# Cache pages of a paged attention in a ring of six group buffers instead of seven

## The reference

```python
PAST_LEN, PAGE_SIZE, DEC_BATCH = 2048, 128, 8
N_HEADS, KV_LORA, QK_ROPE = 8, 512, 64

def mla_sample_attn(q_abs, q_pe, c_new, kpe_new, c_pool, kpe_pool, page_table, w_uv):
    c_past = c_pool[page_table].reshape(dbs, -1, KV_LORA)
    kpe_past = kpe_pool[page_table].reshape(dbs, -1, QK_ROPE)
    s_past = (einsum('bqhr,bkr->bhqk', q_abs, c_past)
              + einsum('bqhe,bke->bhqk', q_pe, kpe_past)) * SOFTMAX_SCALE
    ...
    w = softmax(concatenate([s_past, s_new], axis=-1))
    o_lat = einsum('bhqk,bkr->bqhr', w[..., :n_past], c_past) + einsum(..., c_new)
    return einsum('bqhr,rhv->bqhv', o_lat, w_uv)
```

## Time and profile before

| | us |
|---|---|
| runs before: median of 3 (lowest to highest) | 1185.36 (1183.1 to 1186.95) |
| profiled execution, its own time | 1187.33 |
| its span, first to last instruction | 1185.6 |
| PE busy | 1095.9 |
| DVE, ACT, POOL busy | 590.3, 384.8, 139.0 |
| mean granted PE clock (share of full speed) | 0.971 |

### The profile page before, as it was taken

How to read it: one execution, slowest core, us unless ns; L and a number is a source line. 1 busy time by engine, 2 the same in 40 slices (tenths; PEclk the granted TensorE clock), 3 DMA queues, 4 the chain that set the end, 5 groups by cost and what they waited for, 6 DMA issues and landing times.

```text
span 1185.6 us, 25393 instructions
## 1 busy us (share of the span) xinstructions
PE 1095.9 (92%) x9906; PEld 1016.8 (86%) x9906; DVE 590.3 (50%) x1245; ACT 384.8 (32%) x761; POOL 139.0 (12%) x220
## 2 busy tenths in 40 slices
PE   2899949999999999999789989899999989999995
PEld 2899949999999999989789987677767668999995
DVE  5466432543288851367675436655555552232332
ACT  6331111121133221144551231445444442232333
POOL 0000020000050000010421710123322200000000
PEclk9899978999999999999899989999999999999998
DMA  9443493233344344135535864657777687323213
GB/s 272 100 128 97 127 104 84 76 91 90 90 129 124 98 135 123 63 106 181 157 117 155 256 191 149 204 170 230 219 208 224 197 254 252 107 71 103 74 35 144
DMA packets 199445, 169.99 MB, mean 143 GB/s; under 512 B 35595, under 2 KB 164022, under 8 KB 197526
## 3 DMA queue, kind: packets, MB, share of 16 engines
q1 hardware_dynamic: 177398, 120.51, 36.3%
q0 software_dynamic: 10464, 27.93, 8.9%
q10 hardware_dynamic: 11496, 20.36, 4.9%
HBM read 141.49 MB, written 24.91 MB: 140 GB/s over the span
## 4 chain that ended last, share of the span: by engine, by line
PE 85%; DVE 4%; issue 3%; ACT 3%; DMA 2%; POOL 1%; ACTq 0%; SPq 0%; DVEq 0%; POOLq 0%
PE gemm L1972 12%; PE gemm L1973 12%; PE gemm L1974 12%; PE gemm L2336 5%; PE gemm L2338 5%; PE gemm L2337 5%; PE misc L2248 4%; PE gemm L2288 3%; PE gemm L2267 3%; PE misc L2234 2%; PE misc L2048 2%; PE misc L1999 1%; PE misc L2058 1%; PE misc L1919 1%; DMA gbc<-g_norm 1%
## 5 line engine op out<-in xcount | busy, mean ns | idle before, releaser
L1972 PE MATMUL gemm<-xh,w_hi 128*128 128x260 f32 (+2 forms) x1056 | 303.2, 287 | 0.4 <-DVE w_lo L1263 0.4
L1973 PE MATMUL gemm<-xl,w_hi 128*128 128x260 f32 (+2 forms) x1056 | 301.4, 285 | 0.0
L1974 PE MATMUL gemm<-xh,w_lo 128*128 128x260 f32 (+2 forms) x1056 | 300.6, 285 | 0.0
L1263 DVE TENSOR_TENSOR w_lo<-w_raw,w_hi 128x2048 fp32r<-128x2048 f32 (+3 forms) x65 | 114.4, 1760 | 234.7 <-ACT w_hi L819 232.9
L1972 PEld LDWEIGHTS gemm<-xh,w_hi 128*128 128x128 f32 x1056 | 199.5, 189 | 1.2 <-DVE w_lo L1263 0.6
L1974 PEld LDWEIGHTS gemm<-xh,w_lo 128*128 128x128 f32 x1056 | 199.8, 189 | 0.0
L819 ACT ACTIVATE w_hi<-w_raw 128x2048 fp32r<-128x2048 f32 (+3 forms) x63 | 90.7, 1439 | 336.0 <-PE gemm L1974 295.2
L1973 PEld LDWEIGHTS gemm<-xl,w_hi 128*128 128x128 f32 x1056 | 199.6, 189 | 0.0
L2336 PE MATMUL gemm<-comb_hi,w_hi 128*128 128x260 f32 x512 | 147.1, 287 | 1.1 <-DVE comb_lo L1852 1.1
L2338 PE MATMUL gemm<-comb_hi,w_lo 128*128 128x260 f32 x512 | 144.8, 283 | 0.0
L2337 PE MATMUL gemm<-comb_lo,w_hi 128*128 128x260 f32 x512 | 144.7, 283 | 0.0
(11 more groups left out here) (368 smaller groups left out, 2028.6 us busy)
## 6 DMA issues: line engine op xcount, KB each, us to landing
w_raw<-w_in SPq DMA_DIRECT2D x35, 1024.0 KB, 6.2
ckv<-cache_ckv POOLq DMA_DIRECT2D x72, 256.0 KB, 3.5
w_raw<-w_out SPq DMA_DIRECT2D x16, 1024.0 KB, 5.9
ckv<-cache_ckv SPq DMA_DIRECT2D x56, 256.0 KB, 3.1
z_d<-ev ACTq DMA_DIRECT2D x16, 260.0 KB, 2.1
w_raw<-w_glu SPq DMA_DIRECT2D x8, 512.0 KB, 4.6
yt<-x_prompt SPq DMA_DIRECT2D x4, 1024.0 KB
o_y_p<-yt SPq DMA_DIRECT2D x4, 1024.0 KB
```

Source lines behind the costliest of these rows:

```text
L1263: dve.tensor_tensor(w_lo[:, slot, 0:width], w_raw[:, slot, 0:width], w_hi[:, slot, 0:width].bitcast(F32), ALU.subtract).then_inc(w_lo_read ...
L1972: pe.matmul(acc, a, xa, start=k == 0, stop=False)
L1973: pe.matmul(acc, a, xb, start=False, stop=False)
L1974: last = pe.matmul(acc, b, xa, start=False, stop=k == k_tiles - 1)
```

## The change

The ring gets six slots. The slot at R1 + 18432 goes, and the order of the others changes: groups 2 and 3 of every six now lie at R1, groups 4 and 5 at A0 + 25728. Group i reuses the slot of group i - 6. The ring loads therefore start at group 6, which is even and POOL's; SP keeps the odd groups from 7 on. Of the first six, POOL loads 2 and 3 early (they lie where 4 and 5 lay), then 0 and 1, and 4 when the values are done; SP then loads 5. The early load of group 6 goes, with its wait for the mixing. The wait ahead of `comb_hi` counts group 27 where it counted 26, since 27 is now the last group at R1. What PE, DVE and ACT do, and in which order, is the same but for the slots that they read. The same 32 groups are loaded.

```diff
--- before.py
+++ after.py
@@ -171,7 +171,7 @@
         za = at("za", EV0, [P, 2, NQ])
         ghi = at("ghi", EV0, [P, 2, T], F32R)
 
-        SLOT_AT = (A0, A0 + 9216, A0 + 25728, A0 + 34944, R1, R1 + 9216, R1 + 18432)
+        SLOT_AT = (A0, A0 + 9216, R1, R1 + 9216, A0 + 25728, A0 + 34944)
         ckv = [at(f"ckv{i}", a, [P, 4, KV_LORA]) for i, a in enumerate(SLOT_AT)]
         kpe = [at(f"kpe{i}", a + 8192, [P, 4, QK_ROPE]) for i, a in enumerate(SLOT_AT)]
         cnew = at("cnew", A0 + 22656, [P, KV_LORA])
@@ -319,7 +319,7 @@
         o_gated = sem("o_gated")
         cnt_saved = sem("cnt_saved")
         table_loaded = sem("table_loaded")
-        page_loaded = [[sem(f"page_loaded_{q}{s}") for s in range(7)] for q in ("pool", "sp")]
+        page_loaded = [[sem(f"page_loaded_{q}{s}") for s in range(6)] for q in ("pool", "sp")]
         sample_loaded = sem("sample_loaded")
         wuk_t_ready = sem("wuk_t_ready")
         wuk_t_copied = sem("wuk_t_copied")
@@ -440,7 +440,7 @@
 
         def by_sync(i):
 
-            return i == 3 or (i >= RING and i % 2 == 1)
+            return i == RING - 1 or (i >= RING and i % 2 == 1)
 
         def loads_of(i):
 
@@ -639,7 +639,7 @@
             load_rotary(1)
             sp.wait_ge(table_loaded, 16)
             sp.wait_ge(v_ready, 10)
-            load_group(sp, 3)
+            load_group(sp, 5)
             for u in range(2):
                 sp.wait_ge(v_stored[u], 16 * 5)
             for h in range(2):
@@ -676,7 +676,7 @@
             sp.wait_ge(scores_ready, N_TILES - 4)
             for j in range(2):
                 load_out(j, j)
-            sp.wait_ge(opv_done, pages_freed(26))
+            sp.wait_ge(opv_done, pages_freed(27))
             sp.dma_start(comb_hi[:, 0:8, N_META:T].bitcast(F32), g_d.rearrange("(k p) t -> p k t", p=P)[:, :, N_META:T]).then_inc(glu_loaded, 16)
             sp.wait_ge(sc_ready, N_GROUPS_OF_PAGES)
             sp.wait_ge(unit_ready, len(LAST_USE))
@@ -779,17 +779,15 @@
             pool.wait_ge(state_stored, 16 * 6)
             pool.memset(qa[:, 4:6], 0.0).then_inc(filled, 1)
             pool.wait_ge(table_loaded, 16)
-            for i in (4, 5):
+            for i in (2, 3):
                 load_group(pool, i)
-            pool.wait_ge(gemm_done, B_QN)
-            load_group(pool, 6)
             pool.wait_ge(gemm_done, B_K)
             for i in (0, 1):
                 load_group(pool, i)
             pool.memset(fpad[:], 0.0).then_inc(filled, 1)
             pool.wait_ge(v_ready, 10)
-            load_group(pool, 2)
-            for i in range(RING + 1, N_GROUPS_OF_PAGES, 2):
+            load_group(pool, 4)
+            for i in range(RING, N_GROUPS_OF_PAGES, 2):
                 load_group(pool, i)
 
         @block.scalar
```

## The result

| | before | after |
|---|---|---|
| median of 4 runs each (lowest to highest), us | 1185.36 (1183.1 to 1186.95) | 1228.16 (1223.3 to 1235.95) |
| profiled execution, its own time | 1187.33 | 1235.95 |
| its span | 1185.6 | 1234.2 |
| mean granted PE clock | 0.971 | 0.958 |

The change makes the kernel slower: ratio 1.0369, with a 95% interval of 1.0312 to 1.0426. I had forecast 1200 with a range of 1190 to 1218. The direction was right, the size was not: +42.8 us in the medians where I had +14.4, and +48.6 in the profiled executions. The profiled execution of after was the slowest of its four runs, so sums on its trace are made against 1235.95, not against the median.

The account below looks back on a forecast made before the run. PE, busy 92% of the span, was taken to bound the kernel, loads being bound by slots. Terms 7.3 + 7.0 + 0.1 = 14.4 us took the median of 1185.36 to 1199.8, say 1200, range 1190 to 1218.

Parts of the forecast that it names:

- the end of the ring: Last groups: 0.1 us late before step 30, window 8.4 against need about 8.5; wait before comb_hi 0, high end 2.
- The collision: Before attention, a w_uk load landing late beside page groups, about 4 us; moved, not removed: 0, with -2.5 to +2.5.
- the parts set at 0 or near it: Odd groups 0, ring's end 0.1, wait before comb_hi 0, before attention 0, groups 4 and 5 at attention's start 0.
- the landing: Time from a POOL group's last DMA issue until it lands: 2.9 us at rest, added to 4.76 of issue.
- r=0: Steps 8, 12, ... 28 of attention: need 7.66, window 6.45, late by 1.21 us each, 7.3 in six groups.
- r=2: Steps 6, 10, ... 26, beside head loads: five groups late by 1.26 us, group 26 by 0.72, 7.0 in all.
- The windows: Time from weigh_pages' end in step n-2 to turn_rope(n): 7.24 us at r=2, 7.20 r=3, 6.45 r=0, 10.90 r=1.
- the loads collide harder: Rival, chance 0.12: POOL lands in 6.3 us in step 4k, five groups late by 3.8; +27 us, 1212.
- The issue: POOL's even groups: 4.76 us from the slot's freeing to the start of the eighth DMA.
- The clock rival: Chance 0.14: same 14.4 us, but the granted clock halves after gaps; 20 us at worst, 1220; half of them, 1210.
- 1.2 us is shorter than both: Argument against a clock fall: expected gaps of 1.2 us are shorter than earlier ones of 1.92 and 1.86 us.
- +34: High end of the sum: 6 x 1.6 + 5 x 3.8 + 0.7 + 2 + 2.5 us.

Follow-up runs that it names:

- b1_late7: Kernel before with seven slots, but each ring load from group 7 on waits for group i-6 to be weighed, as with six slots; 1230.66 us, ratio 1.0374.
- a3_no_odd: Changed kernel without the odd page groups from 7 on: SP does not load them and PE does not wait for them; 1221.51 us, ratio 1.0301.
- a4_no_heads: Changed kernel, but from head 2 on the loads of values, gate, queries and keys bring only one partition; 1211.58 us, ratio 1.0224.
- a6_weigh_early: Changed kernel, but in three steps of four PE weighs the old group right after the first page is transposed; 1228.48 us, ratio 1.0359.
- a2_split: Changed kernel, but each ring group is loaded half by POOL and half by SP, four DMAs each; 1199.59 us, ratio 1.013.
- a1_filler: Changed kernel, but in even steps from 6 on PE runs 16 small matmuls before waiting for the page group; 1222.17 us, ratio 1.032.
- a5_swap: Changed kernel with the queues exchanged in the ring: SP loads even groups, POOL odd ones; 1207.73 us, ratio 1.0204.

## Why the prediction was wrong

**What held.** PE bounds the kernel, and a shorter ring acts only by making it wait. Gaps in even steps only, ended by a landing, 13 waits of POOL, nothing behind an odd step, nothing at the end of the ring beyond a shift: all as written. Before attention the sum is right as well (the first turn_rope stands at 746.40, 746.02 before), but by luck. The collision was moved, as I had said, onto two w_uk loads that took 7.2 and 5.1 us to land; PE sat for 3.28 us, and 8 us at a clock of 0.57 followed, where before had 1.92 us and 4. A later fall, of 8 us before (from 706 on) and 4 in after, made up for part of it. b1_late7 shows that the moment of freeing is all there is to it. Of the parts set at 0 or near it, only one was worth 2 us: the gap before step 30 is 2.35 us where I had 0.1.

**The step that failed: the landing.** The term of the sum that was too small is the time from the last issue of a group to its landing. I took "4.76 + 2.9" at r=0 and 8.5 in all at r=2. For after the trace gives, from the end of the weighing to the eighth issue and from there to the start of PE:

| groups | to eighth issue, had | measured | landing of the last, had | measured |
|---|---|---|---|---|
| r=0 (8 to 28) | 4.76 | 4.77 to 5.55 | 2.9 | 3.80, 4.90, 4.13, 4.37, 3.51, 4.49; mean 4.20 |
| r=2 (6 to 22) | 4.76 | 4.76 to 5.27 | 3.7 | 5.02, 6.00, 5.14, 5.07, 5.84; mean 5.41 |
| 26 | 4.76 | 4.78 | 3.2 | 2.83 |
| 30 | 8.5 with the landing | 4.77 | | 5.98 |

The gaps came to 34.7 us where I had 14.4. Of the 20.3 us between them the landings are 6 x 1.30 + 5 x 1.71 - 0.4 = 16.0, group 30 adds 2.2, and the issue adds 12 x 0.25, or 2.9: 21.1. The windows were 0.07 us wider than reckoned, 6.52 at r=0 and 7.30 at r=2 in the mean, which takes 0.8 off. The landing was too small for one reason, seen from two sides.

First, *it is the last DMA that came late*, and PE waits for the last. Landings of group 8 and of group 12 in after, on POOL's line 457 (min, median, max):

```profile
DMA to landing us min/median/max: 2.5/3.3/3.8
```

```profile
DMA to landing us min/median/max: 2.5/3.0/4.9
```

The medians of the two groups, 3.3 and 3.0, look like the 3.0 of the earlier trace rows on which I had built. The eighth DMA took 3.8 and 4.9, the one ahead of it on this line less than 3.6 in both. The trace of before could not have shown this: in its seven POOL groups without such neighbours (first DMA at 798 to 933 us) the eighth landed in 2.7 to 3.1 us. The 2.9 was right for what it was read from, and the 6.7 of the earlier trace rows belongs to a group right behind SP's page and head loads. What failed was to carry the 2.9 over to a place with other neighbours.

Second, *the neighbours were put too far away*. For r=0 I wrote that SP's odd group would be 5.3 to 6.1 us off. That looked back only. The next odd group starts before this one is down; POOL's eighth DMA of group 8, whose landing let PE go at 806.09, and SP's first of group 9:

```profile
802.29 0.54 POOL L457 DMA_DIRECT2D kpe<-cache_kpe  x1
```

```profile
803.07 0.33 SPq L456 DMA_DIRECT2D ckv<-cache_ckv  x1
```

a3_no_odd puts this at 0.7 us for groups 8 to 24, with a wide spread, and at 0.4 with group 28; a4_no_heads takes 0.5 off the same six groups. So for r=0 the late landing is measured, and what share of it each neighbour has stays open. For r=2 I reckoned with a full pipe and 2.47 MB, which gave 3.7 us behind the last issue. Then a4_no_heads shows 3.22 without the head loads, and after 5.41 with them. SP's queue in after at that place, and POOL's first DMA of group 6:

```profile
779.25 0.39 SPq L621 DMA_DIRECT2D vraw<-v_d  x1
781.24 0.43 SPq L611 DMA_DIRECT2D hraw<-q_d  x1
782.19 1.10 SPq L616 DMA_DIRECT2D hraw<-qp_d  x2
787.52 0.35 SPq L456 DMA_DIRECT2D ckv<-cache_ckv  x1
```

```profile
781.85 0.54 POOL L456 DMA_DIRECT2D ckv<-cache_ckv  x1 [29.20 <-PE gemm L2286]
```

The head loads were issued from 779.25 to 783.3, not from 778.5 at once, so they run with POOL's group, whose first DMA is the row of 781.85, and not ahead of it. The rival "the loads collide harder" (0.12) had this cause, but a price of 6.3 us at r=2 alone; the truth lay between it and the sum (5.41), with r=0 late as well.

**The issue.** 4.76 us was one group's value. In after five of the twelve took 5.08 to 5.55, POOL being held inside the group for 0.2 to 0.7 us by "issue", as here in group 14:

```profile
853.43 0.54 POOL L457 DMA_DIRECT2D kpe<-cache_kpe  x1 [0.35 <-issue]
```

The trace names no reason.

**The clock rival (0.14) came true as well.** "1.2 us is shorter than both" stood on the gaps being 1.2 us. All but one were 2.0 to 3.6, above the 1.92 us that had halved the clock, so the argument that kept this case small fell with the landing. It was weak already. The trace of before has a shorter gap with a fall behind it, which the prediction passes over; another of 0.85 us stands 2.5 us ahead of it (PE's timeline, then busy time by stretch):

```profile
707.49 0.80 PE L2175 MATMUL gemm<-w_hi,cn_hi 128*128 128x512 f32 x1 [1.47 <-DVE ev L1626]
...
708.00:710.00 2.00, 2.00 (x6) 1.53 (x5) 0.08 (x1) 2.00 (x2) 0.00 (x0) 0.50 0.37 140
```

And in a6_weigh_early the clock fell behind a gap of 1.69 us, at step 6. The rival's price, 1.7 us a gap, was right: 8 of them are 13.6 us. The two rivals were not independent: harder collisions make longer gaps, and behind 8 of the 12 long ones the clock fell. I had given each a time of its own (1210 and 1212) and none for both together. The prediction's price for the first and its 1.7 us for each of the eight falls that came give 1212 + 8 x 1.7 = 1226, 2 us from the median; that it is eight was known only afterwards. The high end of the costs alone ("+34") was 1219, and the range was cut below it, at 1218, with the clock left out.

**A rule that bears on it.** The Trainium skill, page Perfetto Trace Analysis, section Optimization Strategy, says that a like gap repeated on the engine that should be saturated can mean that there is no room for the next tile, so too few buffers. The trace agrees: 13 gaps before one line, 34.7 us, and one slot more removes them all.

**What stays open.** What made the r=0 groups land late, beyond the 0.4 to 0.5 us that each of the two runs took off. Why the clock stayed up behind the gap of 3.15 us at step 12 and not behind that of 2.46 at step 6. Why the four runs of after lie 12.7 us apart when those of before lie within 4; the mean clock of the other three was 0.960 to 0.964, that of the profiled one 0.958, which goes the right way and is too little to be the whole of it. Why group 20 lands late with neither neighbour. And what the three longer executions of a2_split lost.

## What to carry to other kernels

Whether a ring is deep enough is a comparison of two times: from the last reader of a slot to the first reader of what comes into it, against all issues of that load plus the landing of its *last* DMA, with the neighbours that will be in flight then, those that start later among them. A landing read where the queue has other neighbours is no measure of it: here 2.9 us was right in one place and became 4.2 and 5.4 in another, and since every lack repeats in each turn of the ring, one slot of seven cost 3.7%. An edit of two lines that lets each load wait one group longer, the ring left as it is, shows the loss before any slot is given up (b1_late7: 1.0374 against 1.0369). And look at what the waiting engine does next: of PE's twelve gaps of 2.0 to 3.6 us eight were billed 1.7 us more by the clock, one of them twice that, so a forecast of gaps needs a case in which they are longer and the clock falls too.

## What the runs showed of the hardware

- The granted clock halved behind gaps of PE of 1.47 and 1.92 us (before), 1.69 (a6_weigh_early), and in after 1.79, 2.46, 2.79, 2.86, 2.88, 3.07, 3.44, 3.52 and 3.62 us. It did not behind 1.86 (before), 2.04, 2.25, 2.35 and 3.15 (after), 2.83 (b1_late7) and 2.94 (a3_no_odd). The length alone doesn't decide. About 1.9 us of small matmuls ahead of the wait kept it at 1.00 all through the attention (a1_filler).
- The 32 KB rotary page at the end of a train of eight DMAs on POOL landed in 2.7 to 3.1 us with nothing beside it in before. In after it took 3.5 to 4.9 with the other queue's group starting behind it, and 5.0 to 6.0 beside 1.3 MB of head loads; in a3_no_odd, with neither, 2.8, 3.0, 3.2, 3.4 and once 4.8 us. The DMAs were not full on average, and over the loop they moved less than before (clock, DMA share, GB/s last; after, then before):

```profile
780.00:998.00 218.00, 180.66 (x2042) 133.29 (x2040) 95.16 (x231) 78.55 (x212) 55.97 (x104) 0.93 0.60 176
```

```profile
780.00:950.00 170.00, 165.73 (x2037) 120.88 (x2034) 93.30 (x229) 77.57 (x212) 51.57 (x96) 1.00 0.75 220
```

- POOL needs 4.77 us from the end of the releasing matmul to its eighth DMA (0.7 until the first, then 0.58 each), and at times up to 5.55. SP gets eight out in 3.9 us at its best, and in after took 3.8 to 4.9. Changing the queues over, and with them the order of pages and head loads, was worth 20 us here (a5_swap).
